# Values ahead of the first head's transposes in the attention stretches of a hybrid decoder trunk

## The reference

```python
p_m2, p_s5, p_dsa, p_hg = jnp.split(h @ w_in[l], IN_SPLITS, axis=-1)
y_a, y_b = mamba2_branch(...), s5_branch(...)
y_c, y_d = dsa_branch(...), hgrn2_branch(...)
proj = jnp.einsum("blgc,gcd->blgd", ys, w_branch[l])
x = x + jnp.einsum("blgd,blgd->bld", gates, proj) @ w_out[l]
```

```python
logits = jnp.einsum("bqhd,bqkhd->bhqk", qb, k_sel) * att_scale
prob = jax.nn.softmax(jnp.where(valid[:, None], logits, -jnp.inf), axis=-1)
return jnp.einsum("bhqk,bqkhd->bqhd", prob, v_sel)
```

## Time and profile before

| | |
|---|---|
| median of 3 runs | 2751.54 us (2751.1 to 2751.74) |
| the profiled execution | 2753.97 us, span 2752.2 us |
| PE busy | 2745.2 us (100%), 16054 matmuls |
| PE weight loads | 2337.4 us (85%), beside the matmuls |
| DVE busy | 1844.5 us (67%) |
| ACT busy | 1335.7 us (49%) |
| POOL busy | 940.7 us (34%) |
| logits, line 1043 | 128 matmuls |
| transposes, line 1062 | 160 matmuls |
| values, line 1077 | 320 matmuls |
| granted TensorE clock, mean | 0.999 |

### The profile page before, as it was taken

One profiled execution on the slowest core, in us unless ns is written; L12 is line 12 of the kernel. 1 busy time (PEld: TensorE's weight loads), 2 busy tenths in 40 slices (PEclk: granted clock), 3 DMA queues, 4 the chain that ended last, 5 costly groups with the idle time before them and its releaser, 6 DMA issues.

```text
span 2752.2 us, 41841 instructions
## 1 busy us (share of the span) xinstructions
PE 2745.2 (100%) x16054; PEld 2337.4 (85%) x16054; DVE 1844.5 (67%) x2984; ACT 1335.7 (49%) x2103; POOL 940.7 (34%) x466
## 2 busy tenths in 40 slices
PE   9999999999999999999999999999999999999999
PEld 7898888777788888898988988887777888898988
DVE  6676857785657448585785878577856674585755
ACT  6353444656355446353563534446553653553533
POOL 0134824433343442131121357244333434421221
PEclk9999999999999999999999999999999999999999
DMA  5333584222222233232332335832222222323322
GB/s 171 99 104 123 148 179 115 77 77 70 85 85 84 86 94 99 92 116 99 109 108 92 116 115 155 174 108 80 74 75 79 86 85 85 100 97 95 108 98 102
DMA packets 113109, 284.80 MB, mean 103 GB/s; under 512 B 35616, under 2 KB 45344, under 8 KB 112416
## 3 DMA queue, kind: packets, MB, share of 16 engines
q1 hardware_dynamic: 112928, 282.35, 34.4%
HBM read 268.67 MB, written 9.44 MB: 101 GB/s over the span
## 4 chain that ended last, share of the span: by engine, by line
PE 97%; DVE 2%; DMA 1%; issue 0%; ACT 0%; SPq 0%; ACTq 0%; DVEq 0%
PE bank L622 22%; PE bank L624 21%; PE bank L623 21%; PE bank L671 7%; PE bank L672 7%; PE bank L673 7%; PE bank L648 1%; PE bank L650 1%; PE bank L649 1%; PE bank L1043 1%; PE bank L812 1%; PE bank L1062 1%; PE bank L1077 1%; PE bank L1176 1%; DVE da_s L2786 0%; DMA da_s<-da_qk 0%
## 5 line engine op out<-in xcount | busy, mean ns | idle before, releaser
L477 POOL TENSOR_TENSOR w_lo<-raw,w_hi 128x1024 fp32r<-128x1024 f32 x208 | 520.2, 2504 | 873.3 <-ACT w_hi L469 873.3
L622 PE MATMUL bank<-h_hi,w_hi 128*128 128x512 f32 x1504 | 593.4, 395 | 0.4 <-DVE silu_a L2358 0.3
L624 PE MATMUL bank<-h_hi,w_lo 128*128 128x512 f32 x1504 | 585.9, 390 | 0.0
L623 PE MATMUL bank<-h_lo,w_hi 128*128 128x512 f32 x1504 | 585.8, 389 | 0.0
L469 ACT ACTIVATE w_hi<-raw 128x1024 fp32r<-128x1024 f32 x310 | 326.4, 1056 | 362.5 <-PE bank L624 314.5
L542 POOL TENSOR_TENSOR w_lo<-raw,w_hi 128x1024 fp32r<-128x1024 f32 x122 | 223.5, 1853 | 805.0 <-DVE bank L2303 805.0
L622 PEld LDWEIGHTS bank<-h_hi,w_hi 128*128 128x128 f32 x1504 | 282.3, 188 | 65.2 <-issue 6.7
L624 PEld LDWEIGHTS bank<-h_hi,w_lo 128*128 128x128 f32 x1504 | 282.3, 188 | 59.7
L623 PEld LDWEIGHTS bank<-h_lo,w_hi 128*128 128x128 f32 x1504 | 282.6, 188 | 56.5
L622 PE MATMUL bank<-g_hi,w_hi 128*128 128x512 f32 x698 | 271.9, 390 | 0.0
L623 PE MATMUL bank<-g_lo,w_hi 128*128 128x512 f32 x698 | 271.7, 389 | 0.0
(11 more groups left out here) (452 smaller groups left out, 5892.5 us busy)
## 6 DMA issues: line engine op xcount, KB each, us to landing
raw<-in_w_lots SPq DMA_DIRECT2D x478, 512.0 KB, 3.7
s_wd<-s_z SPq DMA_DIRECT2D x8, 512.0 KB, 2.7
s_t<-s_taps SPq DMA_DIRECT2D x16, 256.0 KB, 13.4
da_s<-da_qk SPq DMA_DIRECT2D x16, 256.0 KB, 4.1
x<-in_x SPq DMA_DIRECT2D x8, 256.0 KB, 5.6
raw_k<-in_w_lots SPq DMA_DIRECT2D x8, 256.0 KB, 6.4
s_w_im<-s_wd SPq DMA_DIRECT2D x32, 64.0 KB, 4.0
s_w_re<-s_wd SPq DMA_DIRECT2D x32, 64.0 KB, 2.8
```

Of the source, the lines that this page charges most:

```text
L477: eng.tensor_tensor(w_lo[:, s], raw[:, s], w_hi[:, s].bitcast(f32), SUB).then_inc(S["lo_done"], 1)
L622: pe.matmul(b[:, :], w_hi[:, s, kw], xh[:, k], start=(k == 0), stop=False)
L623: pe.matmul(b[:, :], w_hi[:, s, kw], xl[:, k], start=False, stop=False)
L624: return pe.matmul(b[:, :], w_lo[:, s, kw], xh[:, k], start=False, stop=(k == nk - 1))
```

## The change

In each stretch TensorE gets the values of the previous pair first, and then the transposes of head 0. The instructions, their waits and the other engines' queues are the same.

```diff
             def att(u):
-                turn(u, 0)
                 if u:
                     values(u - 1)
+                turn(u, 0)
                 if u + 2 < PAIRS:
                     logits(u + 2)
                 turn(u, 1)
```

## The result

The new order takes 2755.08 us (median of 22 runs, 2754.3 to 2757.61) against 2751.31 us (22 runs of the kernel before beside them, 2750.76 to 2752.58): 3.8 us or 0.14% slower, ratio 1.0014 with a 95% interval of 1.0009 to 1.0020. That is inside the 0.2% that the forecast called no change, but the interval leaves out 1, so the loss is real. The forecast was 2755.8 us, 4.3 us slower.

The account below looks back on a forecast made before the run. TensorE's own queue was taken to bound the kernel; 1.26 + 0.33 + 0.59 - 0.02 = 2.16 us a layer, 4.3 us in two, gave 2755.8 us from a median of 2751.54, range 2753.6 to 2757.8.

Parts of the forecast that it names:

- TensorE's queue alone counts, and each change of shape costs at its entry: TensorE ends the chain for 97%; only its queue time counts, each array shape change costs some 0.09 us.
- Products to V: Values entering behind the last large product: 0.08 us more than transposes in that place.
- T behind V: Head 0's transposes behind the values: 0.06 us more for a block of four, 0.03 for a single one.
- T to L: From head 0's transposes to the logits: 0 more than values to logits; at most one more entry of 0.09 us.
- the dearer second switch: Rival, chance 0.12: logits behind late transposes pay one more 0.09 us in 13 pairs of both layers; 2758.1 us.
- The copy between T0 and T1: ScalarE's copy between both heads' transposes: 0, with 0.06 us either way in pairs 0, 1, 4 and 5.
- Pair 13: Values wait for bank 7's splits and transposes no longer fill that time: 0.59 us more a layer.
- The rival without this wait: Rival, chance 0.09: ScalarE gets to y_hi earlier, so pair 13 costs 0.14 us as the others; 2754.9 us.
- Pairs 5 and 9: The other two waits of the values, for da_o and y_lo, have room, so no stall appears there.
- Pairs 14 and 15: No logits there: both heads' transposes become one block of eight, shape changes stay at two; -0.01 us each.
- The sum: All terms together: 2.16 us a layer, 4.3 us in two, 2755.8 us, slower by 0.16%; chance 0.72.
- The rival of hidden entries: Rival, chance 0.07: the values' weights load under the last large product, so only pair 13 loses; 2752.4 us.

Follow-up runs that it names:

- both experiments on it: New order with pair 13 back in the old order: 2754.79 us; new order with ScalarE's y_hi ahead of pair 14's exponentials: 2754.31 us; kernel before 2751.46.
- the two whole-array kernels: Values as 128*128 matmuls with both heads' columns as weights (output differs), old order 2764.13 us, new order 2764.19, against 2751.81 for the kernel before.
- the one with the values last: Order of head 0's transposes, logits, values, head 1's transposes, against the kernel before: 2769.03 us against 2751.81, ratio 1.0063.

## Why the prediction was right, step by step

- **TensorE's queue alone counts, and each change of shape costs at its entry.** Right. With V in the shape of its neighbours the same reordering costs nothing in pair 12.
- **Products to V, 0.08 us.** 0.32 against 0.24 us in the rows (before rounding 0.318 or 0.319 against 0.230 to 0.233), in pairs 1 to 12, 14 and 15; in pair 13 the wait hides it.
- **T behind V, 0.06 us for several transposes, 0.03 for one.** Right for several. For one it was too small: T to L takes 0.26 us in pair 1 (542.07 to 542.33 below) against 0.20 in pair 0. The late start of a block costs 0.06 us even if it has one matmul.
- **T to L at no further cost.** Right: 0.20 us from the last transpose to L in all pairs from 4 on. This was the step without a row, and the rival that hung on it, the dearer second switch at 2758.1 us, falls.
- **The copy between T0 and T1, 0 with 0.06 either way.** It gained in pairs 1, 4 and 5: T1 comes 0.31 us after the start of L's last matmul in place of 0.38. Behind the transposes ScalarE's copy starts 0.04 us after their end, behind V 0.11 (TensorE and ScalarE of pair 4 below, V's end at 563.06, T0's at 563.43, the copy at 563.47). The swap of the two waits shows that it is a matter of which wait ends last: the code waits for the transposes first and for V second, and a release by the second wait costs 0.06 to 0.07 us more than one by the first. In the new order the transposes end last, so the release comes from the first wait. That was not foreseen. In pairs 4 and 5 a third of the gain goes again, since T1's second matmul comes later.

```profile
542.07 0.33 PE L1062 MATMUL bank<-con,da_p 128*128 128x128 f32 x1
542.33 0.49 PE L1043 MATMUL bank<-da_qk 64*128 64x128 f32 x4
...
562.62 0.44 PE L1077 MATMUL bank<-da_pt,da_v 128*64 128x128 f32 x4
562.99 0.44 PE L1062 MATMUL bank<-con,da_p 128*128 128x128 f32 x2
563.36 0.70 PE L1043 MATMUL bank<-da_qk 64*128 64x256 f32 x4
564.00 0.43 PE L1062 MATMUL bank<-con,da_p 128*128 128x128 f32 x2
...
563.47 0.38 ACT L2025 ACTIVATE da_pt<-bank 128x256 f32<-128x256 f32 x1 [2.73 <-PE bank L1062]
```

- **Pair 13, 0.59 us.** 0.589 in each layer, and both experiments on it found the wait where it was put. The rival without this wait falls. Pairs 5 and 9 have none.
- **Pairs 14 and 15, -0.01 each.** -0.006; T0 and T1 are one block of eight:

```profile
648.09 0.39 PE L624 MATMUL bank<-h_hi,w_lo 128*128 128x512 f32 x1
648.41 1.09 PE L1077 MATMUL bank<-da_pt,da_v 128*64 128x128 f32 x16
649.43 1.09 PE L1062 MATMUL bank<-con,da_p 128*128 128x128 f32 x8
```

- **The sum.** 2.17 us a layer against 2.16. By terms: pairs 4 to 12 1.25 (1.26 forecast), pairs 1 to 3 0.35 (0.33), pair 13 0.59 (0.59), pairs 14 and 15 -0.01 (-0.02). That the sum comes within 0.02 us is luck: pairs 1 to 3 were put 0.03 to 0.04 us too cheap each for the single transpose and the rounded starts, pairs 4 to 12 0.01 each, and against both stands the copy's gain of 0.16 us in pairs 1, 4 and 5.
- **The rival of hidden entries** falls on the weight load's row: it starts with V while the shapes differ, and beside the product when they agree.

The medians moved by 3.8 us where the stretches give 4.3, and in the two whole-array kernels and the one with the values last they moved by 0.8 to 1.0 us less than the stretches as well. Part of it is the large products between the stretches: from the first logits to the end the changed kernel takes 4.06 us more than the kernel before, and the other three 12.8, 13.2 and 17.9 us more (12.3, 12.4 and 17.2 by the medians). What is left, 0.3 to 0.8 us, stays open. The start of the program, where the granted clock differed between profiled executions, may be the reason; it wasn't tested.

What an entry's 0.09 us is made of stays open. TensorEngine Tiling (Array Packing) in the Trainium skill, Key Properties, says that changing the tiling mode drains TensorE; the rows agree with it (0.318 us against 0.230 at a change, 0.228 with V over the whole array), but a drain and weights that can't be loaded ahead start at the same moment here, and no run separates them.

## What to carry to other kernels

When a queue of matmuls bounds the kernel, write down the array shape of each block and count the changes: here an order that puts a block next to one of its own shape saves 0.09 us at the entry and 0.06 behind it, 0.15 us a stretch. Check each change against the starts, since a row's shape alone can mislead (the last point below). Put work that is ready ahead of work that may wait, since whatever stood in front of a wait was free. And read starts from row to row: neither the busy share nor one pair of profiled spans shows such a loss at its size.

## What the runs showed of the hardware that was not expected

- ScalarE's copy stands behind two waits. If the event that comes last is the one of the first wait, the copy starts 0.04 to 0.05 us after it (transposes last in the changed kernel, V last in the kernel with the waits swapped); if it is the one of the second wait, 0.10 to 0.11 us (V last in the kernel before). So here the wait for the latest event belongs first; whether that holds for other engines wasn't tried.
- A block of one matmul behind a change of shape delays the next block by 0.06 us, as a longer block delays its own second matmul (0.26 against 0.20 us from a single transpose to the logits).
- The late entry isn't special to the attention. In the trace of the kernel before, blocks of 32*128 (line 1235), 128*64 (line 1176), 64*64 (line 962) and 128*32 (line 854) start 0.318 or 0.319 us after the start of the last large product, and a block of 128*128 (line 1243) starts 0.228 us after it.
- A row's shape doesn't tell by itself whether there is a change. The transposes of line 1114 carry 128*64 as V does, yet they start 1.03 us behind the start of a V of 16, as T and L do after a change, and the next large product starts 0.028 us after their last matmul, as behind T (0.20 us behind the narrow blocks of lines 1176, 1235 and 962). Both would fit an array that isn't split for these transposes; that wasn't tested:

```profile
2037.37 1.09 PE L1077 MATMUL bank<-da_pt,da_v 128*64 128x128 f32 x16
2038.40 0.63 PE L1114 MATMUL bank<-con,m_dp 128*64 128x128 f32 x4
```
